# Turning the rows of x in halves around the fourth accumulator, and opening the next stage's first two weight tiles by blocks of rows

## The reference, cut to what matters

```
for i in range(4):
    h = rms_norm_2(x, norm_mix[i])          # x * rsqrt(mean(x*x) + eps) * gain
    x = x + mixer_i(h)                      # retention, conv, stick breaking, retention
    x = x + squared_relu_mlp(rms_norm_2(x, norm_ffn[i]), w1[i], w2[i])   # relu(h @ w1)**2 @ w2
```

## Time and profile before

| | us |
|---|---|
| median of 3 runs (lowest, highest) | 2092.98 (2092.33, 2095.19) |
| the profiled execution, its own time | 2095.53 |
| its span | 2094.2 |
| PE busy in the span | 1973.4 (94%) |
| DVE, ACT, POOL busy | 1318.0 (63%), 1041.0 (50%), 89.5 (4%) |
| mean granted clock of PE, share of full | 0.974 |
| share of the chain that ended last: PE, DVE, ACT, DMA, issue | 81%, 9%, 5%, 3%, 2% |

### The profile page before, as it was taken

The page is one execution under the profiler, slowest core; times in us unless marked ns, Lnnn a source line. Parts: engine busy times, 40 slices in busy tenths (PEclk is TensorE's granted clock), DMA queues, the critical chain, the costliest instruction groups (busy, mean ns, idle before and its releaser), DMA issues.

```text
span 2094.2 us, 29108 instructions
## 1 busy us (share of the span) xinstructions
PE 1973.4 (94%) x12289; PEld 1738.3 (83%) x12289; DVE 1318.0 (63%) x1596; ACT 1041.0 (50%) x1215; POOL 89.5 (4%) x42
## 2 busy tenths in 40 slices
PE   7799989899989999999988999999999999999998
PEld 2678888698979888899877899897799988888997
DVE  1557764577886466655697665646656575567654
ACT  2657764477764355434535433446443354555332
POOL 0390000000000000000000000000000000000000
PEclk9899999899999999999999999999999999999999
DMA  6681125398964535555530465551356555345562
GB/s 228 247 283 58 61 73 189 128 307 298 310 227 164 183 123 170 172 185 186 163 121 20 147 196 183 183 181 61 101 189 194 186 177 175 127 161 176 186 189 83
DMA packets 230059, 355.55 MB, mean 170 GB/s; under 512 B 7057, under 2 KB 179882, under 8 KB 229674
## 3 DMA queue, kind: packets, MB, share of 16 engines
q1 hardware_dynamic: 229378, 353.47, 51.3%
q10 hardware_dynamic: 552, 0.22, 0.0%
HBM read 352.62 MB, written 1.05 MB: 169 GB/s over the span
## 4 chain that ended last, share of the span: by engine, by line
PE 81%; DVE 9%; ACT 5%; DMA 3%; issue 2%; SPq 1%; POOL 0%; ACTq 0%; DVEq 0%
PE bank L573 12%; PE bank L574 12%; PE bank L575 12%; PE bank L590 11%; PE bank L591 11%; PE bank L592 11%; DVE wlo L1731 3%; ACT whi L1225 2%; PE bank L1082 2%; DVE ARENA L2325 1%; DMA raw<-in_hg_w_in 1%; PE bank L652 1%; ACT ARENA L1236 1%; PE bank L852 1%; DMA raw<-in_moe_w_gate 1%
## 5 line engine op out<-in xcount | busy, mean ns | idle before, releaser
L1731 DVE TENSOR_TENSOR wlo<-raw,whi 128x2048 fp32r<-128x2048 f32 x282 | 658.5, 2337 | 348.5 <-ACT whi L1225 348.1
L1225 ACT CAST whi<-raw 128x2048 fp32r<-128x2048 f32 x282 | 536.6, 1905 | 235.2 <-PE bank L575 210.4
L590 PE MATMUL bank<-HH,whi 128*128 128x256 f32 (+1 forms) x2048 | 605.9, 296 | 15.4 <-DVE HL L1778 9.4
L591 PE MATMUL bank<-HL,whi 128*128 128x256 f32 (+1 forms) x2048 | 597.8, 292 | 0.0
L592 PE MATMUL bank<-HH,wlo 128*128 128x256 f32 (+1 forms) x2048 | 597.5, 292 | 0.0
L590 PEld LDWEIGHTS bank<-HH,whi 128*128 128x128 f32 x2048 | 397.3, 194 | 27.8 <-issue 14.0
L591 PEld LDWEIGHTS bank<-HL,whi 128*128 128x128 f32 x2048 | 397.5, 194 | 8.9 <-issue 1.9
L592 PEld LDWEIGHTS bank<-HH,wlo 128*128 128x128 f32 x2048 | 397.0, 194 | 5.1
L573 PE MATMUL bank<-whi,YH 128*128 128x512 f32 x816 | 321.6, 394 | 10.8 <-DVE YL L2369 5.6
L574 PE MATMUL bank<-wlo,YH 128*128 128x512 f32 x816 | 319.2, 391 | 0.0
L575 PE MATMUL bank<-whi,YL 128*128 128x512 f32 x816 | 318.1, 390 | 0.0
(11 more groups left out here) (355 smaller groups left out, 1921.3 us busy)
## 6 DMA issues: line engine op xcount, KB each, us to landing
raw<-in_ffn_w SPq DMA_DIRECT2D x128, 1024.0 KB, 5.5
raw<-in_ret_w_in SPq DMA_DIRECT2D x48, 1024.0 KB, 5.2
raw<-in_hg_w_in SPq DMA_DIRECT2D x20, 1024.0 KB, 5.4
ARENA<-in_w_mod SPq DMA_DIRECT2D x16, 1024.0 KB, 7.5
raw<-in_ret_w_out SPq DMA_DIRECT2D x16, 1024.0 KB, 4.9
raw<-in_moe_w_gate SPq DMA_DIRECT2D x13, 1024.0 KB, 6.5
raw<-in_moe_w_up SPq DMA_DIRECT2D x13, 1024.0 KB, 6.9
raw<-in_moe_w_down SPq DMA_DIRECT2D x12, 1024.0 KB, 6.7
```

Source lines behind the costliest of these rows:

```text
L590: pe.matmul(ps, w[0][:, k, c], ah, start=begin, stop=False, skip_group_check=True)
L591: pe.matmul(ps, w[0][:, k, c], al, start=False, stop=False, skip_group_check=True)
L1225: ac.copy(whi[n % NS][:, :], raw[place[i]][:, :]).then_inc(*whi_("w", i))
L1731: ve.tensor_tensor(wlo[n % NS][:, :], raw[place[i]][:, :], f32(whi[n % NS][:, :]), SUB).then_inc(*wlv("w", i))
```

## The change

At six of the eight seams (into ffn 0, ffn 1, sb, ffn 2, ret 1 and ffn 3) the work between the stages is put in another order on PE, DVE and ACT. Two of the eight gain multiplications of a quarter pair go from DVE to ACT: DVE multiplies quarters 0 and 2, ACT quarters 1 and 3, before its own cast. No product, no DMA and no weight tile is added or left out.

- PE turns quarters 0 and 1 of the next stage after the third accumulator (q = 1) and before the fourth (q = 3).
- PE opens the next stage (ffn, ret) with two tiles at once, in blocks of rows: first tile 0 and 1; turn of quarters 2 and 3; first tile 2 and 3; second tile 0 to 3; `rms_rows`; first tile 4 to 7; second tile 4 to 7. In sb the second turn stands after the first of its four `proj_a`.
- DVE's `add_out` becomes add 0, add 2, add 1, `gained(0)`, add 3, `gained(2)`, where `gained` is two multiplications and the low part, after a wait for ACT's cast.
- ACT's `add_out` becomes square 0, square 2, high 0, `gained(1)`, square 1, square 3, high 2, `gained(3)`.
- POOL's two low parts stay. The `take()`s stand where they stood, after all of this.

```diff
+        AFTER = {("ret", 0): ("ffn", 0), "conv": ("ffn", 1), ("ffn", 1): "sb", "sb": ("ffn", 2), ("ffn", 2): ("ret", 1),
+                 ("ret", 1): ("ffn", 3)}
...
+            def part_b(tile, ks, ready):
+                use, b, (i, w) = tile
+                for k in ks:
+                    if k % 2 == 0:
+                        pe.wait_ge(*(vlo, plo)[k // 2 % 2].at("n", ready, k // 2))
+                    for m in range(2):
...
+            def opening(stage, uses):
+                first_tile = open_b(uses[0])
+                part_b(first_tile, (0, 1), stage)
+                turned(stage, (2, 3))
+                part_b(first_tile, (2, 3), stage)
+                second_tile = open_b(uses[1])
+                part_b(second_tile, (0, 1, 2, 3), stage)
+                rms_rows(stage)
+                part_b(first_tile, (4, 5, 6, 7), stage)
+                part_b(second_tile, (4, 5, 6, 7), stage)
...
@@ proj_a @@
                         if end and q < 3:
                             x.then_inc(*prj("acc", stage, q))
+                        if end and q == 1 and stage in AFTER:
+                            turned(AFTER[stage], (0, 1))
...
@@ scalar_program, add_out @@
-                for q in (0, 2, 1, 3):
+                def square(q):
...
+                square(0)
+                square(2)
+                st = AFTER.get(stage)
+                if st is not None:
+                    high(st, 0)
+                    gained(st, 1)
+                square(1)
+                square(3)
+                if st is not None:
+                    high(st, 2)
+                    gained(st, 3)
...
+            def gained(st, q):
+                if q == 1:
+                    ac.wait_ge(*plo.at("n", BEFORE_NORM[st], 3))
+                b = banks.of("norm", st, q)
+                ac.wait_ge(*trn.at("norm", st, q))
+                for m in range(2):
+                    k = 2 * q + m
+                    ac.mul(FT[:, k, :], bank[b][:, 256 * m:256 * m + 256], gains(st)[:, k:k + 1]).then_inc(
+                        *aps("ft", st, q))
+                banks.free(("norm", st, q), aps)
+                ac.wait_ge(*aps.last())
+                ac.copy(H8[0][:, 2 * q:2 * q + 2, :], FT[:, 2 * q:2 * q + 2, :]).then_inc(*ahi("n", st, q))
...
@@ vector_program, add_out @@
+                st = AFTER.get(stage)
                 for q in (0, 2, 1, 3):
+                    if q == 3 and st is not None:
+                        gained(st, 0)
                     ve.wait_ge(*prj.at("acc", stage, q))
...
+                if st is not None:
+                    gained(st, 2)
...
+            def gained(st, q):
+                kk = slice(2 * q, 2 * q + 2)
...
+                ve.wait_ge(*trn.at("norm", st, q))
+                for m in range(2):
+                    k = 2 * q + m
+                    ve.tensor_scalar(FT[:, k, :], bank[b][:, 256 * m:256 * m + 256], gains(st)[:, k:k + 1], None,
+                                     MUL).then_inc(*vps("ft", st, q))
+                banks.free(("norm", st, q), vps)
+                ve.wait_ge(*ahi.at("n", st, q))
+                ve.tensor_tensor(H8[1][:, kk, :], FT[:, kk, :], f32(H8[0][:, kk, :]), SUB).then_inc(*vlo("n", st, q))
...
@@ stick, on PE @@
-                norm("sb", X, BEFORE["sb"], late=True)
...
                     proj_a(("sb", "v"), H8, 2 * j, j == 0, j == 3)
+                    if j == 0:
+                        turned("sb", (2, 3))
```

More of the change, by code:

```diff
@@ L438, in build, with gains @@
                   "sb": ("ffn", 1), ("ffn", 2): "sb", ("ret", 1): ("ffn", 2), ("ffn", 3): ("ret", 1)}
+        AFTER = {("ret", 0): ("ffn", 0), "conv": ("ffn", 1), ("ffn", 1): "sb", "sb": ("ffn", 2), ("ffn", 2): ("ret", 1),
+                 ("ret", 1): ("ffn", 3)}
+        def gains(st):
+            if st == "sb":
+                return prm("norm_mix_2", 16, 8)
+            return prm("norm_ffn_2", 8 * st[1], 8) if st[0] == "ffn" else prm("norm_mix_2", 24 * st[1], 8)
         BEFORE_NORM = dict(BEFORE)
@@ L594, in proj_b, with open_b, turned @@
                 prj.also("b", use)
+            def open_b(use):
+                b = banks.next(pe, RING, "b", use, 0)
+                return use, b, take()
+            def part_b(tile, ks, ready):
[4 more added lines that the diff above has]
+                    for m in range(2):
+                        ps, c = bank[b][:, 256 * m:256 * m + 256], slice(128 * m, 128 * m + 128)
+                        ah, al = H8[0][:, k, :], H8[1][:, k, :]
+                        pe.matmul(ps, w[0][:, k, c], ah, start=k == 0 and m == 0, stop=False, skip_group_check=True)
+                        pe.matmul(ps, w[0][:, k, c], al, start=False, stop=False, skip_group_check=True)
+                        x = pe.matmul(ps, w[1][:, k, c], ah, start=False, stop=k == 7, skip_group_check=True)
+                if k == 7:
+                    x.then_inc(*prj("item", i))
+                    prj.also("b", use)
+            def turned(stage, qs):
+                before = BEFORE[stage]
+                for q in qs:
+                    pe.wait_ge(*xr.at("x", before, q // 2))
+                    pe.wait_ge(*xr.at("x", before, 2 + q // 2))
+                    b = banks.next(pe, RING, "norm", stage, q)
+                    for m in range(2):
+                        for i in range(2):
+                            k = 2 * q + m
+                            x = pe.transpose(bank[b][:, 256 * m + 128 * i:256 * m + 128 * i + 128],
+                                             X[i][:, 128 * k:128 * k + 128], ident)
+                    x.then_inc(*trn("norm", stage, q))
+            def opening(stage, uses):
[8 more added lines that the diff above has]
+                part_b(second_tile, (4, 5, 6, 7), stage)
             def proj_a(stage, acts, k0, begin, end):
@@ L993, in ffn @@
                 st = ("ffn", i)
-                norm(st, X, BEFORE[st], late=True)
+                early = st in AFTER.values()
+                if early:
+                    opening(st, [(st, 0), (st, 1)])
+                else:
+                    norm(st, X, BEFORE[st], late=True)
                 for j in range(17):
-                    if j < 16:
+                    if j < 16 and not (early and j < 2):
                         proj_b((st, j), ready=st if j == 0 else None)
@@ L1017, in squares @@
                     x.then_inc(*mm("squares", i, h8))
-                for h8 in range(8):
+                early = st in AFTER.values()
+                if early:
+                    opening(st, [(st, "qk", 0), (st, "qk", 1)])
+                    squares(0)
+                else:
+                    norm(st, X, BEFORE[st], late=True)
+                for h8 in range(2 if early else 0, 8):
                     proj_b((st, "qk", h8), ready=st if h8 == 0 else None)
@@ L1497, in ffn @@
                 st = ("ffn", i)
-                norm(st, H8, late=True)
+                if st not in AFTER.values():
+                    norm(st, H8, late=True)
                 for j in range(17):
@@ L2202, in ffn @@
                 st = ("ffn", i)
-                norm(st, prm("norm_ffn_2", 8 * i, 8), None, H8, BEFORE[st], late=True, ft_free=BEFORE_NORM[st])
+                if st not in AFTER.values():
+                    norm(st, gains(st), None, H8, BEFORE[st], late=True, ft_free=BEFORE_NORM[st])
                 for j in range(16):
@@ L2223, in ret @@
                 st = ("ret", i)
-                norm(st, prm("norm_mix_2", 24 * i, 8), None, H8, BEFORE[st], late=True, ft_free=BEFORE_NORM[st])
+                if st not in AFTER.values():
+                    norm(st, gains(st), None, H8, BEFORE[st], late=True, ft_free=BEFORE_NORM[st])
                 ve.wait_ge(*retc[i].all(1))
```

11 lines of the change are left out of this document (8 added, 3 removed).

## The result

The changed kernel takes 2106.14 us (median of 4 runs, 2104.65 to 2106.83) against 2094.01 for the kernel before (4 runs, 2092.33 to 2095.19): ratio 1.0056, 95% interval 1.0044 to 1.0069. It is slower by 12 us (12.1, or 0.56%, clear of the noise by the interval), and the forecast was 2106.2. Its profiled execution took 2106.83, with a span of 2105.5, 11.3 more than before.

What follows compares the result with a forecast made beforehand. PE, busy 94%, was taken as the bound, with time to win only where it idles or runs at low clock. 2095.5 + 7.8 (seams) + 5.4 (clock) = 2108.7, less 2.5 for the median: 2106.2 us; range 2090 to 2111.

Steps and rivals of the forecast that it cites:

- The step it rested on: At seams with a scale: the seam moves exactly as much as the scale, +1.82 us at ret 0 into ffn 0.
- The chain: From PE's first turn to ACT's weight cast at a seam: nine steps, 7.70 us against 5.88 before.
- step 8: ACT's two gains of quarter 3 in the opening: 0.87 us, taken from a similar activation for lack of a row.
- The 4.97 behind the cast: From the start of ACT's weight cast to the scale on PE: 4.97 us, taken as unchanged.
- The clock: Behind the scale at five seams: three falls to the half clock at 1.8 us each, +5.4 us.
- Nearer to the idle that fell: Ground for three falls: expected 3.1 us idle at the scale lies nearer to 3.7, which fell, than 1.7.
- Costed at nothing: Tail of each opening, later splits and SP's queue: no cost; y(0) at most 2.5 us per ffn without cover.
- The first block: PE's first block of the next tile: about 2.9 us after the first turn (2.86 in the sum).
- -0.05: Seam ffn 1 into sb, no scale: first product 0.93 us earlier, second turn 0.88 behind it, together -0.05.
- the scale does not bind: Rival at `rms_rows` in the opening: idle ahead of the scale is saved, 7.9 us faster, 2085.1; chance 0.15.
- Both nearly cancel: Rival at the seams: chain 1.4 us shorter than added up and clock holds, 0 to +4, about 2095; chance 0.12.
- the clock holds: Rival behind the scales: chain right, no clock falls, 2100.8 us; part of the slower case, which has chance 0.73.

Runs made afterwards that it cites:

- 1: Changed kernel with the norm scale's sum, root and reciprocal ahead of the next weight tile's cast and split in ffn and ret: 2089.08 us, ratio 0.997.
- 2: Kernel before the change with the norm scale computed ahead of the coming weight tile's cast and split: 2088.22 us, ratio 0.9966.
- 6: Changed kernel with one line moved: PE spreads the scale after the last four blocks of the first tile: 2090.14 us, ratio 0.9983.
- 10: Changed kernel with the new order only at the seam from ffn 1 into sb, other seams as before: 2094.78 us, ratio 1.0006.
- 7: Changed kernel with the scale ahead of the weight tile and the last weight split of four stages behind DVE's adds: 2084.72 us, ratio 0.9955.
- 8: Kernel before with the scale ahead of the weight tile and the last weight split of four stages behind DVE's adds: 2084.02 us, ratio 0.9953.
- experiment 5: Changed kernel with 12 extra identity matmuls on PE ahead of its wait for the scale at five seams: 2102.96 us, ratio 1.0047.

## Why the prediction was right, step by step

- **The step it rested on** (a seam moves by as much as its scale) is shown by 1, 2, 6 and 10: cover or advance the scale, and the loss is gone; where there is no scale, there is no loss that could be measured.
- **The chain** was 7.70 and is 8.10. ACT begins 0.91 after DVE's gains, not 0.79 (834.59 - 833.68), and this stands in the chain twice; half of a group of four leaves out the hand-over. DVE begins 0.74 after the first turn, not 0.64 (833.68 - 832.94), though behind the second turn the 0.64 was met. DVE's low part begins 0.65 after ACT's cast, not 0.56 (835.24 - 834.59), and blocks 0 and 1 took 1.50, not 1.45 (837.58 - 836.08). The other steps give back 0.08. ACT's gains (step 8), the one operation without a row, came out as taken: 840.52 - 839.65 = 0.87. The 4.97 behind the cast is exact. The seams therefore give 9.7 for 7.8 us forecast.
- **The clock.** Three falls of five, as forecast, at 1.36, 1.53 and 1.48 where I took 1.8: 4.4 for 5.4. The 1.8 was the difference of 7.60 and 5.80 us, a stretch at 0.73; these ran at 0.78. That it was three is luck: idle pieces of 3.09, 3.08 and 3.09 us fell, 3.00 and 3.18 did not, so the length of a piece does not decide. The kernel before could have told: its slow tile, from which the 1.8 came, stood behind no piece of 3.7 us but behind two of 1.64 and 1.58 with eight turns between them (1166.21 in the earlier trace rows, and the row of 1168.86 above). "Nearer to the idle that fell" was no ground for a count. The Trainium skill (TensorE: Matmul & The Clock Gate, Part 1: The HAM clock gate) lets the clock halve after idling. The trace agrees in direction: the three falls behind a scale each follow such a piece, but two such pieces had none.
- **Not forecast:** 3.0 us less in other stages, half of it a clock fall of before, in sb, that did not come again. Against the profiled execution I forecast +13.2 and it was +11.3. The median agreed to 0.1 by luck: +2.1 at the seams (1.9 of it at the scales), -1.0 at the falls and -3.0 elsewhere met a median that stands 0.7 below the profiled execution of the changed kernel, where I had carried over 2.5. What the runs bear out is the mechanism and a seam's cost to about 0.4 us.
- **Costed at nothing:** y(0) was not waited for, and no wait of PE at a seam names a DMA. The first block came 836.08 - 832.94 = 3.14 after the first turn, 0.28 more than said, by the same three hand-overs. It lies ahead of the idle time, and its wait (0.68) costs nothing by itself; but blocks 0 and 1 start with it and stand in ACT's chain. In sb the first product came 3.05 after the first turn (1358.95 - 1355.90), and the seam gave +0.18 for -0.05.
- **The rivals.** That the scale does not bind is what experiments 1 and 6 make true on purpose: 2089 and 2090, not the 2085.1 that I worked out for it. I had let the seams gain what PE gains; the profile of experiment 1 shows the adds (1.55 us ahead of the first turn) as the next limit, and with them gone too (7 against 8) the halves still gain nothing that can be measured. "Both nearly cancel" and "the clock holds" are out by the chain of 8.10 and the three falls; experiment 5 shows what the second would have given, 2103.0, where 2100.8 was said. What is left open is the 3.0 us elsewhere: no run isolates it.

## What to carry to other kernels

Before reordering the work of the engine that idles, follow the last wait of each stall back through the queues: here a reciprocal of 0.2 us stood behind 4.2 us of weight conversion that could wait (no wait for a weight tile appeared when it did), and every microsecond that the new order put ahead of that queue came out at the end. Put the small operation that an engine waits for ahead of the bulk work of the same queue, or ask for it later; each took 16 to 18 us from the reordered kernel here, and the reordering itself, freed of that queue, nothing that could be measured. A reordering that loses is best undone from both sides: the same repair on the old kernel tells whether the new order is worth anything.

## What the hardware showed unexpectedly

A product of two 128 x 128 fp32 identities cost 0.223 us on PE and counts as two matmuls in the profile, a turn of the same shape 0.11: one cannot stand in for the other as a filler. And idle pieces within 0.2 us of each other in length ended with the low clock in three cases and without in two, while 12 such fillers in the same places kept it at 1.00 behind all five.

The clock also fell at a seam without any long idle piece, in the kernel before at conv into ffn 1: 1.64 and 1.58 us of waiting with eight turns between them were followed by the half clock. In the changed kernel, with 3.00 us of waiting ahead of the turns and again ahead of the scale, it did not fall there.
